# A decoder step with 32 streamed experts: the overflow branch moved between experts, and an ending of its own for the last one

## What is computed

```python
logits = u @ w_router + b_router
top_val, top_idx = lax.top_k(logits, TOP_K)            # 4 of 32
gates = jax.nn.softmax(top_val, axis=-1)
# for the rows that chose expert e, each with its gate:
gu = xb @ w_gu[e] + b_gu[e]                             # 1024 -> 2048
gate = jnp.minimum(gu[:, :D_FF], SWIGLU_LIMIT)
lin = jnp.clip(gu[:, D_FF:], -SWIGLU_LIMIT, SWIGLU_LIMIT)
act = (lin + 1.0) * gate * jax.nn.sigmoid(SWIGLU_ALPHA * gate)
y += gates * (act @ w_down[e] + b_down[e])              # 1024 -> 1024
# at the end
h = h + y
out = h * rsqrt(mean(h * h) + EPS) * g_final
```

## Time and profile before

| what | value |
|---|---|
| time of three runs, median (lowest to highest) | 1184.42 us (1181.4 to 1185.86) |
| time of the profiled execution | 1181.74 us |
| its span, first to last instruction | 1180.0 us |
| TensorE busy | 1116.6 us, 95% of the span |
| VectorE busy | 353.1 us, 30% |
| ScalarE busy | 194.8 us, 17% |
| read from HBM | 421.59 MB, mean 359 GB/s |

### The profile page before, as it was taken

One profiled execution on the slowest core, in us unless ns is written; L12 is line 12 of the kernel. 1 busy time (PEld: TensorE's weight loads), 2 busy tenths in 40 slices (PEclk: granted clock), 3 DMA queues, 4 the chain that ended last, 5 costly groups with the idle time before them and its releaser, 6 DMA issues.

```text
span 1180.0 us, 13853 instructions
## 1 busy us (share of the span) xinstructions
PE 1116.6 (95%) x5336; PEld 475.9 (40%) x5336; DVE 353.1 (30%) x655; ACT 194.8 (17%) x309; POOL 13.9 (1%) x35
## 2 busy tenths in 40 slices
PE   4999999999999999999999999999999999999994
PEld 2776775433333333333333333333333333333331
DVE  4642423312222222332222222222222222222224
ACT  2221532111111111111111111111111111111112
POOL 4000000000000000000000000000000000000000
PEclk9997869999999999999999999999999999999997
DMA  8710317379999999999999999999999999999992
GB/s 277 284 37 1 143 43 308 146 304 426 425 427 427 427 427 427 427 427 427 426 427 427 426 427 427 427 426 426 426 427 427 426 427 427 425 427 426 427 398 75
DMA packets 51918, 424.16 MB, mean 359 GB/s; under 512 B 7386, under 2 KB 12064, under 8 KB 19100
## 3 DMA queue, kind: packets, MB, share of 16 engines
q1 hardware_dynamic: 51048, 423.29, 86.2%
q10 hardware_dynamic: 180, 0.35, 0.1%
q0 software_dynamic: 672, 0.27, 0.1%
HBM read 421.59 MB, written 2.33 MB: 359 GB/s over the span
## 4 chain that ended last, share of the span: by engine, by line
PE 47%; DMA 46%; ACT 3%; DVE 2%; issue 1%; POOL 0%; SPq 0%; DVEq 0%; ACTq 0%; POOLq 0%
DMA raw<-in_w_gu 46%; PE ps L1163 20%; PE ps L1174 7%; PE ps L935 6%; PE ps L1196 2%; PE ps L1140 2%; PE ps L1052 2%; PE ps L1246 1%; PE ps L1016 1%; PE ps L1147 1%; PE ps L1012 1%; PE ps L982 1%; PE ps L1184 1%; DMA raw<-in_gn_b 1%; PE ps L923 1%
## 5 line engine op out<-in xcount | busy, mean ns | idle before, releaser
L1163 PE MATMUL ps<-raw,xT 128*64 128x512 f32 x2048 | 465.2, 598 | 22.8 <-DMA raw<-in_w_gu 22.1
L1163 PEld LDWEIGHTS ps<-raw,xT 128*64 128x64 f32 x2048 | 139.8, 137 | 314.8 <-issue 269.3
L1174 PE MATMUL ps<-raw,actT 128*64 128x512 f32 x1024 | 226.9, 596 | 3.6 <-DVE yacc L890 3.6
L890 DVE TENSOR_TENSOR yacc<-ps,yacc 128x1024 f32<-128x1024 f32 x99 | 115.2, 1217 | 158.8 <-PE ps L1196 145.6
L865 DVE TENSOR_TENSOR hS<-ps,bguT 128x512 f32<-128x512 f32 x64 | 41.2, 686 | 374.6 <-PE ps L1246 374.6
L1174 PEld LDWEIGHTS ps<-raw,actT 128*64 128x64 f32 x1024 | 74.0, 138 | 151.3 <-issue 151.3
L1196 PE MATMUL ps<-yS,GT 64*128 64x512 f32 x384 | 91.1, 606 | 2.2 <-DVE hS L865 1.5
L515 ACT ACTIVATE xr<-ps 128x512 f32<-128x512 f32 x33 | 19.7, 597 | 423.4 <-PE ps L1140 422.4
L1140 PE MATMUL ps<-u,sel 128*64 128x512 f32 x384 | 87.8, 592 | 0.0
L1196 PEld LDWEIGHTS ps<-yS,GT 64*128 64x128 f32 x384 | 34.6, 186 | 57.0 <-issue 56.0
L851 DVE TENSOR_TENSOR sel<-slot_no,pos 128x192 f32<-128x192 f32 x33 | 11.8, 358 | 148.7 <-PE ps L1140 148.7
(11 more groups left out here) (269 smaller groups left out, 579.5 us busy)
## 6 DMA issues: line engine op xcount, KB each, us to landing
raw<-in_w_gu SPq DMA_DIRECT2D x128, 2048.0 KB, 23.4
raw<-in_w_down SPq DMA_DIRECT2D x128, 1024.0 KB, 23.9
wv<-in_w_in SPq DMA_DIRECT2D x3, 2048.0 KB, 19.7
raw<-in_w_in SPq DMA_DIRECT2D x2, 2048.0 KB, 10.8
wv<-in_w_out SPq DMA_DIRECT2D x1, 4096.0 KB, 12.9
wv<-in_state_gla SPq DMA_DIRECT2D x8, 128.0 KB, 2.4
out_gla_s<-wv SPq DMA_DIRECT2D x8, 128.0 KB
yacc<-in_x_prompt SPq DMA_DIRECT2D x1, 512.0 KB
```

The lines of the kernel that those rows point to most:

```text
L890: dve.tensor_tensor(dst, ps[:, PAIR[c]:PAIR[c] + 2, :], dst, ALU.add).then_inc(sem("added"), 1)
L1163: last = pe.matmul(ps[S * w:S * w + S, n, :], xT[:, k % 4, k // 4, :], raw[:, k, col:col + 512], start=(k == 0), stop=(k == KD - 1))
L1174: last = pe.matmul(ps[S * w:S * w + S, 4, :], actT[:, k, :], raw[:, p, col:col + 512], start=(k == 0), stop=(k == KD - 1))
```

## The change

The branch on the flag moves from behind the loop to between expert 23 and expert 24 (`SPLIT = 24`) on TensorE, VectorE, ScalarE and SyncE: a loop over 2 to 23, the flag, the branch with its overflow passes, and a third loop whose body is called with `i + more`, where `more` is the register with the number of overflow passes. That third loop ends with pass 30; pass 31 and what follows it are written out in `finish`.

In `finish` the gather and the row transposes for an expert 32 are gone. TensorE transposes `guS` of expert 31 behind the first of four down pieces of expert 30. The last down weights go to pieces 0 to 3, which the gate-and-up product of expert 31 releases, under two semaphores of their own; `gfin` and `yout` go to pieces 8 to 10. The down product of expert 31 uses bank 0 and an `actT` in the place of `guS`; its gate matrix is transposed into bank 1 between its second and third piece. Both last scatters come at the end, the second accumulating onto the first, so that `yacc` gets one round of three adds instead of two. ScalarE loads the root's table right after the last sigmoid with a root of one column, and squares and takes the root chunk by chunk; VectorE takes the reciprocal and the product chunk by chunk.

The rest of the diff moves the statements of the bodies, unchanged, into functions: `act_of` (L862 to L872), `weigh` (L873 to L877), `act_done` (L878 to L882), `collect` (L889 and L890), `gu`, `dn`, `scatter`, `turn_weights` (L1237 to L1240), `turn_gu` (L1242 to L1247).

```diff
+    SPLIT = 3 * NE // 4
...
-        gfin = flat(raw[:, 0:1, :])[:, 0:D]
-        yout = flat(raw[:, 1:3, :])[:, 0:TC * D].rearrange("p (c d) -> p c d", c=TC)
+        gfin = raw[:, 8, 0:D]
+        yout = flat(raw[:, 9:11, :])[:, 0:TC * D].rearrange("p (c d) -> p c d", c=TC)
         junk = raw[:, 4, 0:D]
+        yS_end = xr
+        GT_end = xT.rearrange("p q h s -> p (q h s)")[:, 0:TC * P]
+        actT_end = guS[:, 0:KD * S].rearrange("p (k s) -> p k s", k=KD)
...
-            with sp.Fori(2, NE) as i:
+            def round_of(i):
                 for p in GU:
                     piece(p, i)
                 for p in DN:
                     piece(p, i - 1)
+
+            with sp.Fori(2, SPLIT) as i:
+                round_of(i)
             sp.wait_ge(sem("flag_ready"), 1)
             over = sp.value_load(flag[0:1, 0:1], min_val=0, max_val=1)
-            last = over * (NV - NE) + NE
             with sp.If(over):
-                with sp.Fori(NE, NV) as i:
-                    for p in GU:
-                        piece(p, i)
-                    for p in DN:
-                        piece(p, i - 1)
+                with sp.Fori(SPLIT, SPLIT + NV - NE) as i:
+                    round_of(i)
+            more = over * (NV - NE)
+            with sp.Fori(SPLIT, NE) as i:
+                round_of(i + more)
+            n = more + (NE - 1)
             for p in DN:
-                sp.wait_ge(sem(f"used{p}"), last - 1)
+                sp.wait_ge(sem(f"used{(p - 8) // 2 * 2}"), n + 1)
                 r = (p - 8) * 2 * P
-                load(raw[:, p, :].rearrange("p (k n) -> p k n", k=2),
-                     A["w_down"][0, NE - 1, r:r + 2 * P, :].rearrange("(p k) n -> p k n", p=P), f"piece_in{p}")
-            sp.wait_ge(sem("used0"), last)
+                load(raw[:, p - 8, :].rearrange("p (k n) -> p k n", k=2),
+                     A["w_down"][0, NE - 1, r:r + 2 * P, :].rearrange("(p k) n -> p k n", p=P), "end_in_a" if p < DN[2] else "end_in_b")
+            sp.wait_ge(sem("used8"), n)
             load(gfin, A["g_final"].rearrange("(a n) -> a n", a=1).broadcast_to([P, D]), "gfin_in")
...
-        def passes(eng, body, load_flag=True):
+        def passes(eng, body, finish):
 
             body(0)
             body(1)
-            with eng.Fori(2, NE) as i:
+            with eng.Fori(2, SPLIT) as i:
                 body(i)
             eng.wait_ge(sem("flag_ready"), 1)
             over = eng.value_load(flag[0:1, 0:1], min_val=0, max_val=1)
             with eng.If(over):
-                with eng.Fori(NE, NV) as i:
+                with eng.Fori(SPLIT, SPLIT + NV - NE) as i:
                     body(i)
-            last = over * (NV - NE) + NE
-            body(last, ahead=False)
-            body(last + 1, ahead=False, between=False)
-            return last
+            more = over * (NV - NE)
+            with eng.Fori(SPLIT, NE - 1) as i:
+                body(i + more)
+            finish(more + (NE - 1))
...
+            def gu_rows(i):
+
+                act.wait_ge(sem("used6"), i + 1)
+                if not isinstance(i, int) or i >= 1:
+                    act.wait_ge(sem("gu_turned"), i)
+                act.activation(guS[:, :].rearrange("p (a n) -> p a n", a=2), ps[:, 0:2, :], ACT.Copy).then_inc(sem("guS_ready"), 1)
+
+            def down_rows(i):
+
+                act.wait_ge(sem("used11"), i)
+                if not isinstance(i, int) or i >= 2:
+                    act.wait_ge(sem("scattered"), TC * (i - 1))
+                act.activation(yS[:, :], ps[:, 4, :], ACT.Copy).then_inc(sem("yS_ready"), 1)
+
+            def finish(n):
+
+                act.wait_ge(sem("clipped"), n)
+                act.wait_ge(sem("product"), n)
+                act.activation(hS[:, 0, :], hS[:, 0, :], ACT.Sigmoid, scale=ALPHA).then_inc(sem("sig_ready"), 1)
+                gu_rows(n)
+                act.wait_ge(sem("clipped"), n + 1)
+                act.wait_ge(sem("product"), n + 1)
+                act.activation(hS[:, 0, :], hS[:, 0, :], ACT.Sigmoid, scale=ALPHA).then_inc(sem("sig_ready"), 1)
+                link(act.activation(small[:, 7:8], eps, ACT.Sqrt))
+                down_rows(n)
+                act.wait_ge(sem("gt_turned"), n)
+                act.activation(GT[:, :], ps[:, 6, 0:TC * P], ACT.Copy).then_inc(sem("GT_ready"), 1)
+                act.wait_ge(sem("gt_turned"), n + 1)
+                act.activation(GT_end, ps[:, 1, 0:TC * P], ACT.Copy).then_inc(sem("GT_ready"), 1)
+                act.wait_ge(sem("used11"), n + 1)
+                act.activation(yS_end[:, :], ps[:, 0, :], ACT.Copy).then_inc(sem("yS_ready"), 1)
+                for c in range(TC):
+                    act.wait_ge(sem("added"), TC * n + c + 1)
+                    act.activation(junk, yacc[:, c, :], ACT.Square, accum_out=ssq[:, c:c + 1]).then_inc(sem("sq2"), 1)
+                    act.wait_ge(sem("sq2"), c + 2)
+                    act.activation(rstd[:, c:c + 1], ssq[:, c:c + 1], ACT.Sqrt, scale=1.0 / D, bias=eps).then_inc(sem("std_h"), 1)
+
+            passes(act, body, finish)
...
-            dve.wait_ge(sem("ssq"), 2 * TC)
-            dve.tensor_scalar(ssq, ssq, 1.0 / D, EPS, ALU.mult, ALU.add).then_inc(sem("var"), 1)
-            dve.wait_ge(sem("std"), 2)
-            link(dve.reciprocal(rstd, rstd))
-            dve.wait_ge(sem("gfin_in"), 16)
-            for c in range(TC):
-                dve.scalar_tensor_tensor(out=yout[:, c, :], in0=yacc[:, c, :], scalar=rstd[:, c:c + 1], in1=gfin,
-                                         op0=ALU.mult, op1=ALU.mult).then_inc(sem("y_ready"), 1)
...
+            def finish(n):
+
+                act_of(n)
+                weigh(n)
+                dve.wait_ge(sem("used11"), n - 1)
+                act_done(n, actT[:, :, :])
+                for c in range(TC):
+                    dve.wait_ge(sem("scattered"), TC * (n - 2) + c + 1)
+                    collect(c)
+                act_of(n + 1)
+                act_done(n + 1, actT_end)
+                weigh(n + 1)
+                for c in range(TC):
+                    dve.wait_ge(sem("scattered"), TC * (n - 1) + c + 1)
+                    collect(c)
+                dve.wait_ge(sem("gfin_in"), 16)
+                for c in range(TC):
+                    dve.wait_ge(sem("std_h"), TC + c + 1)
+                    link(dve.reciprocal(rstd[:, c:c + 1], rstd[:, c:c + 1]))
+                    dve.scalar_tensor_tensor(out=yout[:, c, :], in0=yacc[:, c, :], scalar=rstd[:, c:c + 1], in1=gfin,
+                                             op0=ALU.mult, op1=ALU.mult).then_inc(sem("y_ready"), 1)
+
+            passes(dve, body, finish)
...
+            def dn(i, p, acts, weights, bank, at_end=False):
...
+                if at_end:
+                    pe.wait_ge(sem("end_in_a" if p < DN[2] else "end_in_b"), 32)
+                else:
...
+            def spread_rows(weights, values, start, stop):
+
+                for c in range(TC):
+                    for n in range(2):
+                        last = pe.matmul(ps[:, PAIR[c] + n, :], weights[S * n:S * n + S, c * P:(c + 1) * P], values[S * n:S * n + S, :], start=start, stop=stop)
+                    if stop:
+                        last.then_inc(sem("scattered"), 1)
+
+            def scatter(i):
+
+                pe.wait_ge(sem("yS_ready"), i - 1)
+                pe.wait_ge(sem("GT_ready"), i - 1)
+                pe.wait_ge(sem("biased"), 2 * i)
+                spread_rows(GT, yS, True, True)
+
+            def turn_weights(i, bank):
+
+                pe.wait_ge(sem("gm_ready"), TC * i)
+                for c in range(TC):
+                    last = pe.transpose(ps[:, bank, c * P:(c + 1) * P], Gm[:, c, :], ident[:, :])
+                last.then_inc(sem("gt_turned"), 1)
+
...
+            def finish(n):
+
+                pe.wait_ge(sem("xT_ready"), n + 1)
+                pe.wait_ge(sem("guS_ready"), n)
+                gu(n, 0, 4)
+                scatter(n)
+                gu(n, 4, 8)
+                pe.wait_ge(sem("act_ready"), n)
+                pe.wait_ge(sem("added"), TC * n)
+                dn(n, DN[0], actT, raw[:, DN[0], :], 4)
+                turn_gu(n)
+                for p in DN[1:]:
+                    dn(n, p, actT, raw[:, p, :], 4)
+                turn_weights(n, 6)
+                pe.wait_ge(sem("act_ready"), n + 1)
+                for p in DN:
+                    dn(n + 1, p, actT_end, raw[:, p - 8, :], 0, at_end=True)
+                    if p == DN[1]:
+                        turn_weights(n + 1, 1)
+                pe.wait_ge(sem("yS_ready"), n)
+                pe.wait_ge(sem("GT_ready"), n)
+                pe.wait_ge(sem("biased"), 2 * n + 2)
+                spread_rows(GT, yS, True, False)
+                pe.wait_ge(sem("yS_ready"), n + 1)
+                pe.wait_ge(sem("GT_ready"), n + 1)
+                spread_rows(GT_end, yS_end, False, True)
+
+            passes(pe, body, finish)
```

(70 more changed lines are left out.)

150 lines of the change are left out of this document (45 added, 105 removed).

## The result

The change makes the kernel faster: a median of 1171.93 us (1171.36 to 1176.27, 7 runs) against 1181.4 (1179.16 to 1185.86, 7 runs) for the kernel before beside it, a ratio of 0.9917 with a 95% interval of 0.9896 to 0.9937. The forecast was 9.9 us less, a ratio of 0.9916; its median of 1174.5 us was 2.6 too high, and the median of before is 3.0 us lower over these seven runs than over the three that the forecast started from.

What follows compares the result with a forecast made beforehand. The prediction took weight transfers at 426 GB/s to bound the loop, so only the ending could gain: 8.4 us up to the down product's end plus 1.5 behind it, 9.9 in all, giving 1174.5 us, range 1170.5 to 1180.5.

Steps and rivals of the forecast that it cites:

- The bound and the middle: Expert loop: weights set the pace, TensorE has 1.07 us spare per expert; moving the branch there gains nothing.
- The 1.46 us taken for the branch: TensorE's stop at the moved branch for flag load, compare and jump: 0 to 1.46 us, taken as 1.46.
- the cover of seven passes: Experts 24 to 30: TensorE's spare 1.07 us per pass wins back the branch's delay, up to 7.5 us.
- Rival 2: Third loop pays for an instruction fetch at every pass and the kernel gets slower, 1191.5 us; chance 0.07.
- DMA: Ending: sending the last down weights to pieces 0 to 3 closes a 1.7 us hole in the transfers.
- the 2.0 us for the landing: Ending: TensorE sees the last down weights 2.0 us after their last byte; bounds 0 and twice that.
- TensorE: Ending: the last down product ends at 1155.8 instead of 1164.2 us, a gain of 8.4 us.
- Norm: Ending: the last product ends 11.6 us behind the down product instead of 13.1, a gain of 1.5 us.
- Without that cover it would come back whole: Norm: the root's 1.28 us table load would cost its full time without the 12 us before yS is wanted.
- Rival 1: Ending: TensorE's clock falls after its waits; one drop costs 1.7 us; chance beyond one drop 0.14.
- Sum: Whole kernel: last product at 1167.4 instead of 1177.3 us, 9.9 us less, median 1184.42 becoming 1174.5.

Runs made afterwards that it cites:

- the middle alone: Kernel before with only the new loops and the branch ahead of expert 24, old ending kept: 1183.97 us against 1184.09, ratio 0.9995.
- the late branch: Kernel after with the branch ahead of expert 30 instead of 24, one pass behind it: ending 49.34 us against 49.36.
- the old buffers: Kernel after with the last down weights in pieces 8 to 11 again: ending 49.39 us against 49.36.
- the gather back: Kernel after with the gather for an expert 32 restored: ending 49.43 us; with last down weights in pieces 8 to 11 as well, 52.25.
- bank 0 alone: Kernel before with only expert 31's down product written to bank 0, not waiting for VectorE's adds: ending 54.27 us against 59.36.
- the transposes last: Kernel after with expert 31's gate-and-up result transposed behind all four down pieces of expert 30: ending 52.79 us against 49.36.
- the free buffers alone: Kernel before with only the last down weights moved to pieces 0 to 3, and gfin and outputs moved: ending 57.59 us against 59.36.

## Why the prediction was right, and where it was not

**The bound and the middle.** Right. The loop runs at the pace of the weights; the branch in the middle alone gives 0.9995. The 1.46 us taken for the branch were not its cost but VectorE's, as the middle alone shows: TensorE's wait shrank by 0.09 us, and the late branch shows that the cover of seven passes was not needed. Rival 2 falls: 29.52 us per pass behind the branch, and instruction packets only around the change of loops.

**DMA.** The step had the hole close because the weights go to pieces 0 to 3. The hole closes, but this edit was not needed for it: the old buffers give the same ending, because the missing gather had closed it already. With the gather back the free buffers do close it, as the step said. The times that the step gave hold: weights seen at 29.5 and 34.4 us behind expert 31's start in both forecast (1147.4, 1152.3, less 1117.9) and trace (1151.35, 1156.21, less 1121.85), so the pace and the 2.0 us for the landing were right together.

**TensorE.** Right in its end, 37.9 against 38.01 us, and nearly in the waits. Of the 8.3 us by which the down product ends earlier, bank 0 alone gives 5.1 (3.4 of waiting for VectorE's adds, 1.7 of clock). The other 3.2 go with making actT earlier than the weights, and the transposes behind the first piece are needed for that: their undoing costs 3.4, a pause with half clock in it included. Which edits make up the 3.2 was not shown one by one; the one round of adds instead of two and the missing row transposes for an expert 32 were not undone. The prediction had all of these in its timeline but gave none of them a price of its own.

**Norm.** Right: 11.6 against 11.35 us, and the chunks are worth 1.67 with the table load early in both runs. "Without that cover it would come back whole" was wrong for the table load: 0.71 of 1.28 us come back, as VectorE's three adds are a cover that the prediction didn't see. The root starts 0.02 us behind its load in before and 0.01 in the run without the early load. The drain of about 1.38 us that the Trainium skill (ScalarE: Activation LUTs, What ACT_TABLE_LOAD costs) adds to every switch of tables appears in neither trace, so the prediction was right to go by the row.

**Rival 1.** It did not come, and two experiments show what it would have cost: after 4.16 us without a matmul (the transposes last) the first half product took 1.7 us more, and after 3.95 (the middle alone) the whole product the same 1.7. In the ending of after the longest pause is 2.65 us.

**Sum.** 9.9 us forecast, 10.0 in the endings, 9.5 between the medians. The endings bear out the two terms of the sum: the down product ends 8.3 us earlier (forecast 8.4), and what follows it takes 1.7 less (forecast 1.5). That the ratio agrees to 0.0001 is luck: its interval is 0.4% wide, and of the seven runs of after four lie near 1171.7 us and three near 1176, so that one run more among the latter and one less among the former would have made the median 1175.5. The 10.0 also hold the 1.7 us of half clock in the one trace of before.

## What to carry to other kernels

When a loop runs at the pace of its weights, look for the gain in the ending, and ask of each wait there which shared thing causes it: here one PSUM bank shared with VectorE's adds was half of the change. Two edits that close the same hole don't add up; undo each one alone, and both together, before giving either a price. An engine that waits for transfers in the ending has room for work that now stands behind it, the more so if it can tell the transfers apart.

## What the runs showed beyond that

**The start varies by 4 us.** Ahead of expert 31's start all fourteen traces run the same work or, in the loop, work at the pace of the weights, yet it starts between 1116.9 and 1122.9 us, in two groups: eight at 1116.9 to 1118.6, six at 1121.5 to 1122.9. Most of the difference is there when expert 0's first product starts: at 219.8 to 221.1 us in the eight, at 223.5 to 224.6 in the six. The windows over the token mixing differ in TensorE's mean granted clock, 0.91 in all of the eight and 0.88 or 0.89 in the six; here after (late group) and the old buffers (early group):

```profile
0.00:222.00 222.00, 199.41 (x999) 140.34 (x1000) 88.03 (x231) 65.49 (x106) 13.90 (x35) 0.88 0.40 146
```
```profile
0.00:222.00 222.00, 198.24 (x1009) 138.84 (x1011) 87.92 (x231) 66.08 (x107) 13.90 (x35) 0.91 0.40 146
```

The seven runs of after split the same way, four at 1171.4 to 1171.9 and three at 1175.5 to 1176.3. The clock and the late start go together; what decides them was not tried.

**Two pauses of nearly one length, two clocks.** In the ending TensorE fell to half clock after pauses of 3.64, 3.95 and 4.16 us (before, the middle alone, the transposes last) and did not after one of 3.57 (the free buffers alone), nor, up to the last matmul, in the ten endings with no pause over 2.65. So the 1.7 us may be missing from some executions of before: its 30 runs spread over 7.9 us (1179.16 to 1187.06), the seven of after over 4.9. This is not shown, as those runs have no trace.
